# The end of a mixture-of-experts kernel: gate rows loaded early, the last expert's outputs evicted as two banks and brought back with four row tiles

## The reference

```python
mod = (jax.nn.silu(cond) @ p["w_ada"][i] + p["b_ada"][i])[:, None, :]
sh1, sc1, g1, sh2, sc2, g2 = jnp.split(mod, N_MOD, axis=-1)
...
x = x + g1 * m
h = rms_norm(x, p["norm_ffn"][i]) * (1 + sc2) + sh2
x = x + g2 * moe(h, p["router_w"], p["router_b"], p["moe_w_gate"][i],
                 p["moe_w_up"][i], p["moe_w_down"][i])
return rms_norm(x, p["norm_final"]), ...
```

## Time and profile before

| what | us |
|---|---|
| median of 3 runs | 848.37 |
| lowest, highest | 840.24, 850.57 |
| the profiled execution | 846.58 |
| its span, first to last instruction | 844.9 |
| TensorE busy | 746.5 (88%) |
| VectorE busy | 315.4 (37%) |
| ScalarE busy | 184.3 (22%) |
| mean granted TensorE clock | 0.934 |

### The profile page before, as it was taken

How to read it: one execution, slowest core, us unless ns; L and a number is a source line. 1 busy time by engine, 2 the same in 40 slices (tenths; PEclk the granted TensorE clock), 3 DMA queues, 4 the chain that set the end, 5 groups by cost and what they waited for, 6 DMA issues and landing times.

```text
span 844.9 us, 22586 instructions
## 1 busy us (share of the span) xinstructions
PE 746.5 (88%) x9624; PEld 407.1 (48%) x9625; DVE 315.4 (37%) x806; ACT 184.3 (22%) x390; POOL 40.3 (5%) x97
## 2 busy tenths in 40 slices
PE   5699776768999988999998999999999999999734
PEld 5355462355644466544552653554554554455211
DVE  3889769997013265311211111211201211120138
ACT  3554240201022230021201021201201202120122
POOL 1000000000020001300000000000000000000000
PEclk9989897867999976999999999999999999999976
DMA  8900448970139792599999999999999999999971
GB/s 343 414 27 2 183 174 345 263 289 16 40 116 364 266 358 101 169 400 410 410 410 411 402 406 411 410 410 411 410 410 381 412 410 411 411 410 410 410 299 75
DMA packets 70795, 262.08 MB, mean 310 GB/s; under 512 B 10797, under 2 KB 10845, under 8 KB 66649
## 3 DMA queue, kind: packets, MB, share of 16 engines
q1 hardware_dynamic: 68216, 257.69, 77.8%
q0 software_dynamic: 1552, 2.99, 0.9%
q10 hardware_dynamic: 976, 0.67, 0.5%
HBM read 252.49 MB, written 9.17 MB: 310 GB/s over the span
## 4 chain that ended last, share of the span: by engine, by line
PE 68%; DVE 10%; DMA 9%; SPq 5%; issue 5%; ACT 2%; ACTq 0%; DVEq 0%
PE ps L1188 25%; PE ps L1195 11%; PE ps L1180 8%; DMA ring<-in_moe_w_up 5%; PE ps L1094 5%; SPq L406 3%; PE ps L1154 3%; PE ps L1045 3%; PE ps L947 2%; DMA vreg<-y_scratch 2%; PE ps L987 2%; PE ps L852 1%; DVE sreg L1433 1%; PE ps L1255 1%; PE ps L879 1%
## 5 line engine op out<-in xcount | busy, mean ns | idle before, releaser
L1188 PE MATMUL ps<-ring,vreg 128*32 128x512 f32 x2240 | 248.5, 599 | 13.2 <-DMA ring<-in_moe_w_up 7.4
L1188 PEld LDWEIGHTS ps<-ring,vreg 128*32 128x32 f32 x2240 | 72.7, 111 | 181.9 <-issue 164.7
L1195 PE MATMUL ps<-ring,vreg 128*32 128x256 f32 x2240 | 124.4, 380 | 0.8 <-ACT vreg L808 0.8
L1725 DVE TENSOR_TENSOR vreg<-vreg,ps 128x256 f32<-128x256 f32 x48 | 17.3, 417 | 212.6 <-ACT vreg L803 212.6
L1195 PEld LDWEIGHTS ps<-ring,vreg 128*32 128x32 f32 x2240 | 71.1, 110 | 48.1 <-issue 1.0
L1180 PEld LDWEIGHTS ps<-vreg,sreg 128*128 128x128 f32 x720 | 82.7, 192 | 12.6 <-issue 12.6
L1180 PE MATMUL ps<-vreg,sreg 128*128 128x96 f32 x720 | 86.0, 276 | 0.0
L1739 DVE COPY vreg<-ps 32x256 f32<-32x256 f32 x96 | 40.6, 423 | 99.8 <-PE ps L1195 97.2
L818 ACT ACTIVATE vreg<-ps 32x256 f32<-32x256 f32 x96 | 35.9, 374 | 139.6 <-PE ps L1195 137.6
L803 ACT ACTIVATE vreg<-ps 128x256 f32<-128x256 f32 x48 | 15.0, 384 | 205.0 <-PE ps L1188 205.0
L1094 PE MATMUL ps<-ring 128*128 128x512 f32 x128 | 57.8, 609 | 1.4 <-issue 0.7
(11 more groups left out here) (286 smaller groups left out, 592.2 us busy)
## 6 DMA issues: line engine op xcount, KB each, us to landing
ring<-in_moe_w_down SPq DMA_DIRECT2D x128, 512.0 KB, 12.1
ring<-in_moe_w_gate SPq DMA_DIRECT2D x123, 512.0 KB, 12.9
ring<-in_moe_w_up SPq DMA_DIRECT2D x123, 512.0 KB, 14.0
ring<-in_w_ada SPq DMA_DIRECT2D x24, 1024.0 KB, 9.6
ring<-in_ssm_w_glu SPq DMA_DIRECT2D x8, 1024.0 KB, 16.4
ring<-in_ssm_w_in SPq DMA_DIRECT2D x8, 512.0 KB, 21.6
y_scratch<-sreg SPq DMA_DIRECT2D x6, 512.0 KB, 7.9
tmat<-ada_rows SPq DMA_DIRECT2D x4, 512.0 KB, 9.8
```

The costliest lines, as they stand in the source:

```text
L1188: last = pe.matmul(ps[t][32 * j:32 * j + 32, :], xgT[:, k, 32 * t:32 * t + 32], w[:, :, 256 * j:256 * j + 256], start=(k == 0), stop=(k == ...
L1195: last = pe.matmul(ps[3 + t // 2][32 * dj:32 * dj + 32, 256 * (t % 2):256 * (t % 2) + 256], aT[:, t, c2, 32 * j:32 * j + 32], ring[:, KT + ...
```

## The change

1. The rows of `g2` get a tile of their own, `gate2`, and are loaded early, behind the zeroing of `y2_scratch` and ahead of the state outputs; the loads at the end are gone. One semaphore, `ld_gate`, counts both pairs of rows.
2. The last expert's outputs are copied by ScalarE alone, in two instructions (bank 3 as 128x512, bank 4 as 128x256), in the form in which they stand in PSUM, into `y_last` (which lies in `yrow`). VectorE copies nothing there.
3. The one-hot matrix is written four times, once for each block of 32 partitions, `oh_rep` (twelve ScalarE copies of 32x384 ahead of the loop in the place of one of 96x384). TensorE no longer waits for it ahead of the loop but at the end; the wait ahead of expert 0's `down` covers bank 3.
4. TensorE brings the rows back with 36 matmuls: weights 32x128, 256 columns, four at a time in the four row tiles, each into a bank of its own (`back_banks`), accumulating over the three slot tiles. Token tile 2 uses the other halves of tile 0's banks and waits for `dve_back`, which VectorE raises in `combine(0)`.
5. ScalarE scales tile 0, evicts, and then scales tiles 1 and 2. VectorE does `other_choice` of all three tiles before anything else. `combine` multiplies in four pieces of 128x256 in the place of two of 128x512.
6. ScalarE loads the square-root table ahead of the final norm with a dummy instruction.
7. `dynamic_dma_scratch_size=2048` is given to the program; the argument was absent before. It sets how many bytes of each SBUF partition are kept for GpSimd's DMA descriptors.

```diff
+        gate2 = sb("gate2", [P, 2, D])
+        oh_rep = sb("oh_rep", [P, TT, NT * P])
...
+        y_last = yrow[:, 0:TT * 256].rearrange("p (t n) -> p t n", t=TT)
...
-        ohT_last = sig[0:CAP, 0:NT * P].rearrange("p (t n) -> p t n", t=NT)
+        back_banks = ((0, 1, 2, 5), (6, 7, 3, 4), (0, 1, 2, 5))
+
+        def back_of(t, j):
+            return ps[back_banks[t][j]][:, 256 * (t // 2):256 * (t // 2) + 256]
...
-            sp.wait_ge(pool_zeros, 1)
+            sp.wait_ge(pool_late, 14)
             for t in range(2 * NT):
                 sp.dma_start(y2_d[t * P:(t + 1) * P, :], zeros).then_inc(st_zero, 16)
+            sp.wait_ge(ld_gate, 32)
+            for cond in range(2):
+                load_rows(gate2[:, cond, :], cond, 2, 2, ld_gate)
...
-            for cond in range(2):
-                load_rows(gate_rows[:, cond, :], cond, 2, 2, ld_g2)
             sp.wait_ge(y_sent, 16 * (NE - 1))
...
                 if last:
                     first_choice(0, 1)
-                    first_choice(1, 1)
                 act.wait_ge(unit_free, it * NU + NU)
                 act.wait_ge(y_free, it + 1)
+                if last:
+                    act.activation(y_last[:, 0:2, :], ps[3][:, :].rearrange("p (t n) -> p t n", t=2), ACT.Copy
+                                   ).then_inc(act_y_last, 1)
+                    act.activation(y_last[:, 2, :], ps[4][:, 0:256], ACT.Copy).then_inc(act_y_last, 1)
+                else:
+                    rows_of_slots()
...
-            act.activation(ohT_last, ps[3][0:CAP, 0:NT * P].rearrange("p (t n) -> p t n", t=NT), ACT.Copy
-                           ).then_inc(act_oh_last, 1)
+            for j in range(4):
+                for t in range(TT):
+                    act.activation(oh_rep[32 * j:32 * j + 32, t, :], ps[3][32 * t:32 * t + 32, 0:NT * P], ACT.Copy
+                                   ).then_inc(act_oh_last, 1)
+            act.wait_ge(act_oh_last, 4 * TT)
+            act.sem_inc(y_ev, 1)
...
             expert(NE - 1, True)
+            first_choice(1, 1)
             first_choice(2, 1)
...
             act.nop()
+            act.activation(stat[:, 14:15], ident[:, 0:1], ACT.Sqrt)
...
-            pe.wait_ge(act_oh_last, 1)
             pe.wait_ge(dve_cmax, 1)
...
-            pe.wait_ge(y_ev, 12 * NE + 12)
+            pe.wait_ge(act_oh_last, 4 * TT)
+            pe.wait_ge(act_y_last, 2)
             for t in range(NT):
-                for half in range(2):
-                    last = pe.matmul(ps[2 * t + half][:, :], ohT_last[:, t, :], yrow[0:CAP, 512 * half:512 * half + 512],
-                                     start=True, stop=True)
+                if t == 2:
+                    pe.wait_ge(dve_back, 1)
+                for c in range(TT):
+                    for j in range(4):
+                        a = slice(32 * j, 32 * j + 32)
+                        last = pe.matmul(back_of(t, j), oh_rep[a, c, t * P:(t + 1) * P], y_last[a, c, :],
+                                         start=(c == 0), stop=(c == TT - 1), skip_group_check=True)
                 last.then_inc(pe_back, 1)
...
                 if last:
-                    dve.wait_ge(ld_g2, 32)
-                    other_choice(0, 1)
-                    other_choice(1, 1)
-                dve.wait_ge(unit_free, it * NU + NU)
-                dve.wait_ge(y_free, it + 1)
+                    dve.wait_ge(ld_gate, 64)
+                    for t in range(NT):
+                        other_choice(t, 1)
+                else:
+                    dve.wait_ge(unit_free, it * NU + NU)
+                    dve.wait_ge(y_free, it + 1)
+                    rows_of_slots()
...
-            other_choice(2, 1)
             v = dve.value_load(cmaxi[0:1, 0:1], min_val=0, max_val=T)
...
             def combine(t):
                 dve.wait_ge(pe_back, t + 1)
-                for half in range(2):
-                    c2 = slice(512 * half, 512 * half + 512)
-                    step(tt(x1[:, t, c2], ps[2 * t + half][:, :], gate_rows[:, 1 if t else 0, c2], ALU.mult), half == 1)
+                for j in range(4):
+                    c2 = slice(256 * j, 256 * j + 256)
+                    step(tt(x1[:, t, c2], back_of(t, j), gate2[:, 1 if t else 0, c2], ALU.mult), j == 3)
+                if t == 0:
+                    dve.sem_inc(dve_back, 1)
                 tt(x1[:, t, :], x1[:, t, :], y2c[0][:, t, :], ALU.add).then_inc(dve_x2, 1)
...
-    nc = bacc.Bacc("TRN2", target_bir_lowering=False, num_devices=1)
+    nc = bacc.Bacc("TRN2", target_bir_lowering=False, num_devices=1, dynamic_dma_scratch_size=2048)
```

More of the change, by code:

```diff
@@ L254, in build @@
         dve_done, act_mo = sem("dve_done"), sem("act_mo")
-        st_rows, ld_g1, ld_g2, ld_mod2 = (sem(n) for n in ("st_rows", "ld_g1", "ld_g2", "ld_mod2"))
+        st_rows, ld_gate, ld_mod2 = (sem(n) for n in ("st_rows", "ld_gate", "ld_mod2"))
         ld_y2 = [sem(f"ld_y2_{t}") for t in range(NT)]
@@ L262, in build @@
         st_list, st_out, st_scatter = (sem(n) for n in ("st_list", "st_out", "st_scatter"))
-        pool_zeros, st_zero, dve_oh_last, pe_oh_last, act_oh_last, dve_pre, pe_back, dve_oh_none, dve_mix = (sem(n) for n in (
-            "pool_zeros", "st_zero", "dve_oh_last", "pe_oh_last", "act_oh_last", "dve_pre", "pe_back", "dve_oh_none", "dve_mix"))
+        st_zero, dve_oh_last, pe_oh_last, act_oh_last, dve_pre, pe_back, dve_oh_none, dve_mix = (sem(n) for n in (
+            "st_zero", "dve_oh_last", "pe_oh_last", "act_oh_last", "dve_pre", "pe_back", "dve_oh_none", "dve_mix"))
         ld_early = [sem(f"ld_early{u}") for u in range(len(early_unit))]
@@ L272, in build @@
         y_free, sidx_ready, dve_round = sem("y_free"), sem("sidx_ready"), sem("dve_round")
+        act_y_last, dve_back = sem("act_y_last"), sem("dve_back")
         ticks = [sem("send_tick"), y_free]
@@ L369, in _ @@
             for cond in range(2):
-                load_rows(gate_rows[:, cond, :], cond, 1, 0, ld_g1)
+                load_rows(gate_rows[:, cond, :], cond, 1, 0, ld_gate)
             sp.wait_ge(pe_y, 6)
@@ L519, in _ @@
             assert n[0] == 13
-            pool.memset(zeros, 0.0).then_inc(pool_zeros, 1)
+            pool.memset(zeros, 0.0).then_inc(pool_late, 1)
             pool.dma_start(list_d.rearrange("(p a) v -> p (a v)", p=P), listi).then_inc(st_list, 16)
@@ L829, in _ @@
             with act.If(v > CAP):
+                act.wait_ge(act_y_last, 2)
+                rows_of_slots()
                 with act.Fori(1, ROUNDS) as r:
@@ L1554, in _ @@
             stt(ada[0:64, 2, :], ada[0:64, 2, :], 1.0, gains[0:64, :], ALU.add, ALU.mult).then_inc(dve_ada, 1)
-            dve.wait_ge(ld_g1, 32)
+            dve.wait_ge(ld_gate, 32)
             dve.wait_ge(ld_x_ctx, 16)
@@ L1717, in other_choice @@
                 dve.wait_ge(dve_mix, 2 * (NT * (loads - 1) + t) + 1)
-                tt(m, m, gate_rows[:, 1 if t else 0, :], ALU.mult).then_inc(dve_mix, 1)
+                tt(m, m, gate2[:, 1 if t else 0, :], ALU.mult).then_inc(dve_mix, 1)
                 dve.wait_ge(dve_mix, 2 * (NT * (loads - 1) + t) + 2)
@@ L1730, in expert, with rows_of_slots @@
                 if last:
-                    dve.wait_ge(ld_g2, 32)
-                    other_choice(0, 1)
-                    other_choice(1, 1)
-                dve.wait_ge(unit_free, it * NU + NU)
-                dve.wait_ge(y_free, it + 1)
+                    dve.wait_ge(ld_gate, 64)
[4 more added lines that the diff above has]
+                    dve.wait_ge(y_free, it + 1)
+                    rows_of_slots()
+            def rows_of_slots():
                 for t in range(TT):
@@ L1740, in _ @@
             dve.sem_inc(prod_done, TT)
-            dve.sem_inc(y_ev, 12)
+            dve.sem_inc(y_ev, 11)
             evict_x(0)
@@ L1752, in _ @@
             expert(NE - 1, None, True, True)
-            other_choice(2, 1)
             v = dve.value_load(cmaxi[0:1, 0:1], min_val=0, max_val=T)
             with dve.If(v > CAP):
+                dve.wait_ge(act_y_last, 2)
+                rows_of_slots()
                 with dve.Fori(1, ROUNDS) as r:
@@ L1769, in _ @@
                 dve.wait_ge(dve_pre, 2 * NT)
-                dve.memset(ohT_last, 0.0).then_inc(dve_oh_none, 1)
+                dve.wait_ge(act_oh_last, 4 * TT)
+                dve.memset(oh_rep[:, :, :], 0.0).then_inc(dve_oh_none, 1)
             dve.nop()
```

1 line of the change is left out of this document (added).

## The result

The changed kernel takes 841.24 us (median of 15 runs, 836.51 to 845.64), the kernel before 846.13 us (15 runs, 840.24 to 854.01). The ratio is 0.993, with a 95% interval of 0.9906 to 0.9954: 5.9 us less, 4 to 8 by the interval. Forecast were 842 us and 5.1 us less.

What follows compares the result with a forecast made beforehand. The weight stream was taken to bound the experts, then the landing of tile 0's rows and VectorE the end. Terms -2.56 - 2.70 + 0.45 - 0.30 = -5.1 us gave 841.5 (843.3 from the median); 842 forecast, range 836 to 849.

Steps and rivals of the forecast that it cites:

- Gate rows: End: without 1.05 MB queued ahead of them, the `y2` rows land 2.56 us sooner; bounds 2.23 to 2.56, or 0.
- Rival 1: End: the rows don't land earlier, so the change does half of what it says; 844 us, chance 0.10.
- Copies off VectorE: End: six copies between the second and third `other_choice` leave VectorE's path, -2.70 us.
- smaller pieces: `combine`: four 128x256 pieces take 1.44 us against 1.29 for two of 128x512; three times, +0.45 us.
- the gap kept: Ahead of `combine(0)`: VectorE's 0.36 us, read as its own read of `cmaxi` and branch, stays.
- Ahead of the loop: Loop entry: TensorE no longer waits for L821, gaining between 0 and 0.5 us; 0.3 taken.
- TensorE's way back: End: 72 records start at 813.8, four row tiles together at factor 3.7, off the path.
- Rivals 2 and 3: TensorE's return: row tiles run one at a time, 844 us, chance 0.10; also at 1.2 GHz throughout, 854 us, 0.03.
- Twelve copies: ScalarE ahead of the loop: one-hot copies take some 6 us, to 336.6, before SiLU is wanted; cost 0.
- square-root table: Ahead of the final norm: VectorE was never kept waiting by the table load, so 0.
- descriptor space: GpSimd's sends: 6 us each with some 18 us slack to the next eviction, so 0.
- rival 4: Expert loop: sends become slow with little descriptor space and evictions wait; at 27 us, +39, 881 us; chance 0.01.

Runs made afterwards that it cites:

- regrouped ones: Changed kernel with VectorE's passes on token tiles 1 and 2 regrouped, 839.67 us; the same with TensorE's way back also next to the branch, 836.14 us.
- regrouped, near, again: Changed kernel with VectorE's work on tiles 1 and 2 regrouped and TensorE's way back also next to the branch, one repeat run: 840.27 us.

## Why the prediction was right

Step by step, with the prediction's term and what came of it:

- Gate rows, -2.56: -2.57 in the changed kernel and -2.53 alone. Right, and it is the term of the bytes ahead in a full queue (2.56), not the issue time (2.23), that it meets. Rival 1 is out.
- Copies off VectorE, -2.70, smaller pieces, +0.45, the gap kept: together -2.25; measured 26.45 to 23.93, -2.52 (-2.43 against the mean of three profiles of before). Up to `combine(0)` it is 11.59 us in the place of 14.44: 2.85, not 2.70. From there on it is 12.34 us in the place of 12.01, or of 11.83 where `combine(1)` did not wait for TensorE: the smaller pieces cost 0.5 us. Four of them took 1.42 us where I had 1.44, two took 1.29 before. I had not seen that short wait in `combine(1)`, which the change takes away (0.2 us). The gap stood in every kernel with rounds (0.36 us, and 0.30 in the regrouped ones) and went to 0.03 without, so reading it as VectorE's own branch, against the profile's "PE ps L1294", was right.
- Ahead of the loop, -0.30: mis-sized. It is -0.95, and -0.96 with nothing else changed. My upper bound, the length of L821 (0.49 us), was wrong. The likely reason, by the order of the code, is that the wait also held back TensorE's read of the expert's count and the branch behind it; freed, they run beside VectorE's copy instead of after L821. On top comes the chance that the clock does not fall, 1.70 us of records, of which the runs leave open how much belongs to the change and how much reaches the end.
- TensorE's way back, off the path: right in the end, wrong in the step. I had it start at once behind ScalarE's copies; it came 4.5 us later, in the changed kernel 5.6 us behind `down`, by the same kind of branch that I had seen on VectorE. `other_choice(2)` on VectorE covered it. The row tiles ran together: 24 records in 1.58 us at a clock of 1.00, 66 ns each against 213 one at a time, 3.2 times; 48 in 2.87 us, 3.6 times ("regrouped, near, again", 1.00); and tiles 0 and 1 of the changed kernel took 5.50 us at a clock of 0.50, where I had 5.6. Rivals 2 and 3 are out. The rule of the Trainium skill ("TensorEngine Tiling (Array Packing)", Gotcha 1: PSUM Pressure) about banks was kept by this kernel; no run here breaks it, so none shows its price.
- Twelve copies, square-root table, descriptor space, 0: the copies took 6.04 us and ended 9 us ahead of SiLU; GpSimd's wait for expert 14's send is still 5.2 us (5.20 before, 5.16 after), so rival 4 is out.

Sum of what was measured piece by piece: 2.57 + 2.52 + 0.95 = 6.0 us, and 5.9 by the ratio. The forecast of 5.1 was short by the entry (0.65) and by 0.27 on VectorE. That the ratio meets the sum so well is in part luck: its interval is 4 us wide, and the ratios of the parts taken alone (4.5 us for the gate rows, 4.0 for the entry) add up to more than the whole. The extra 4 us of the two profiled spans are the part ahead of the loop (VectorE's copy ended at 331.31 and 328.90: 2.4 us) and the experts (470.81 and 468.95: 1.9 us, of which the first one's records are 1.7).

## What to carry to other kernels

Where the time is a sum of stages with noise in one of them, compare pieces between fixed marks of the trace: here they repeat to hundredths of a us, where a dozen executions of the whole tell 2 to 3 us. But a piece shows only what lies in it: see that the cost you fear can fall inside one. The price of a wait in front of a loop can be more than the time of what is waited for (0.95 us for a copy of 0.49), as reads and branches stand behind it. Look at "issue" time ahead of a first instruction, and put the common path directly behind its branch; whether that is worth time depends on who is waited for, and here it was VectorE.

## What the runs showed that I had not expected

TensorE needs 5.6 us (5.56 to 5.71 in five profiles) from its last matmul of the loop to the first one behind the skipped rounds, and no more than 2.7 us, when it only waits for its input, where that code stands next to the branch or the rounds are left out (three profiles). The instruction queue moves at that time; in the stretch from 805 to 815 us of the changed kernel's queues:

```profile
q8 instruction: 2, 0.03, 1.4%
```

One of the two comes ahead of TensorE's first matmul. All five profiles with the late start have exactly one there, 2.8 to 3.1 us behind the end of `down` and 2.7 to 2.8 us ahead of the matmul; the three with the early start have none between `down` and the matmul. That speaks for the code being fetched after the jump, though the profile does not say for which engine a transfer is. No run separates how far the jump goes from that there is a jump at all, and VectorE, which jumps over its own rounds, shows a gap of only 0.36 us. The fall of TensorE's clock ahead of expert 0 came in three of thirteen short or middle pauses (1.1 to 2.3 us) and costs 1.7 us in that expert's records when it comes; after 7.8 us of pause it cost 2.55 us.
